# A conditioned two-block transformer layer stack: the first stage in the order of its data, and three weight pieces split a stage earlier

## The reference

```python
mod = silu(c) @ w_ada + b_ada            # 6 vectors of 1024, also for c_ctx
sh1, sc1, gt1, sh2, sc2, gt2 = split(mod, 6)
h  = rms_norm(x, g_norm1) * (1.0 + sc1) + sh1
hc = rms_norm(ctx, g_norm1) * (1.0 + csc1) + csh1
aq, ak, av, dq, dk, dv, dz, da, db, ga, gd = split_cols(h @ w_in)
...                                      # attention; gated delta rule, 12 steps, both directions
y_d = rms_norm(o_d, dn_norm_g) * silu(dz)
y = sigmoid(ga) * (y_a @ w_br_attn) + sigmoid(gd) * (y_d @ w_br_dn)
```

## Time and profile before

| | |
|---|---|
| runs shown | 2957.41, 2962.56, 5729.62 us; median 2962.56 |
| profiled execution | 2958.29 us, span 2956.3 |
| TensorE busy | 2718.9 us, 92% |
| VectorE, ScalarE busy | 49%, 30% |
| mean granted clock of TensorE | 0.96 of full |
| moved by DMA | 242.41 MB, mean 82 GB/s |

### The profile page before, as it was taken

The page is one execution under the profiler, slowest core; times in us unless marked ns, Lnnn a source line. Parts: engine busy times, 40 slices in busy tenths (PEclk is TensorE's granted clock), DMA queues, the critical chain, the costliest instruction groups (busy, mean ns, idle before and its releaser), DMA issues.

```text
span 2956.3 us, 48454 instructions
## 1 busy us (share of the span) xinstructions
PE 2718.9 (92%) x20908; PEld 2170.7 (73%) x20908; DVE 1444.9 (49%) x2474; ACT 892.1 (30%) x1516; POOL 87.2 (3%) x140
## 2 busy tenths in 40 slices
PE   3999988888889999998889899999999889899998
PEld 1767656667778778876767678888888666688876
DVE  2455556668853444434356653333334346544434
ACT  2434421110032333223335432222222335333322
POOL 0000011112200000000000000000000000000000
PEclk6999989999999999999899999999999899999999
DMA  6000356550023223222000212111210100222220
GB/s 250 30 29 29 130 186 230 206 189 3 3 87 121 86 86 110 90 86 82 29 29 29 86 37 78 58 57 58 80 63 29 39 29 29 114 89 111 86 86 29
DMA packets 17921, 242.41 MB, mean 82 GB/s; under 512 B 2016, under 2 KB 2176, under 8 KB 2864
## 3 DMA queue, kind: packets, MB, share of 16 engines
q1 hardware_dynamic: 16416, 231.94, 21.1%
q0 software_dynamic: 1296, 7.39, 0.6%
HBM read 237.23 MB, written 2.10 MB: 81 GB/s over the span
## 4 chain that ended last, share of the span: by engine, by line
PE 86%; DVE 8%; issue 2%; DMA 2%; ACT 2%; POOL 0%; DVEq 0%; ACTq 0%; SPq 0%; POOLq 0%
PE ps L333 57%; PE ps L1221 7%; PE ps L395 2%; PE ps L1778 2%; PE ps L1997 2%; PE ps L875 1%; PE ps L2025 1%; PE ps L2041 1%; PE ps L831 1%; DVE hh L486 1%; PE ps L2043 1%; PE ps L2042 1%; DMA cst<-in_consts 1%; PE ps L877 1%; PE ps L876 1%
## 5 line engine op out<-in xcount | busy, mean ns | idle before, releaser
L333 PE MATMUL ps<-hh,ws 128*128 128x512 f32 x3600 | 856.8, 397 | 39.1 <-DVE hh L486 27.0
L333 PEld LDWEIGHTS ps<-hh,ws 128*128 128x128 f32 x3600 | 679.8, 191 | 199.8 <-issue 46.9
L324 DVE TENSOR_TENSOR ws<-raw,ws 128x1024 fp32r<-128x1024 f32 x295 | 360.2, 1222 | 242.1 <-ACT ws L316 242.0
L316 ACT ACTIVATE ws<-raw 128x1024 fp32r<-128x1024 f32 x295 | 309.3, 1050 | 507.0 <-PE ps L333 433.2
L333 PE MATMUL ps<-g,ws 128*128 128x512 f32 x1536 | 364.5, 395 | 0.0
L333 PEld LDWEIGHTS ps<-g,ws 128*128 128x128 f32 x1536 | 286.1, 188 | 67.2
L1221 PEld LDWEIGHTS ps<-ar 64*64 64x64 f32 x6656 | 214.8, 141 | 52.5 <-issue 34.4
L1532 DVE SCALAR_TENSOR_TENSOR xT<-ps,mods,xT 128x512 f32<-128x512 f32 x120 | 90.1, 750 | 323.3 <-PE ps L333 323.3
L1221 PE MATMUL ps<-ar 64*64 64x64 f32 x6656 | 230.6, 226 | 18.0 <-issue 10.3
L333 PE MATMUL ps<-gg,ws 128*128 128x512 f32 x960 | 226.1, 395 | 0.0
L333 PEld LDWEIGHTS ps<-gg,ws 128*128 128x128 f32 x960 | 180.3, 188 | 43.7
(11 more groups left out here) (313 smaller groups left out, 2997.9 us busy)
## 6 DMA issues: line engine op xcount, KB each, us to landing
raw<-in_w_ada SPq DMA_DIRECT2D x36, 2048.0 KB, 8.6
raw<-in_w_m SPq DMA_DIRECT2D x32, 2048.0 KB, 7.8
raw<-in_w_mlp SPq DMA_DIRECT2D x16, 2048.0 KB, 7.7
raw<-in_w_in SPq DMA_DIRECT2D x8, 2048.0 KB, 7.8
raw<-in_w_mg SPq DMA_DIRECT2D x8, 1536.0 KB, 6.6
raw<-in_w_out SPq DMA_DIRECT2D x6, 2048.0 KB, 7.6
raw<-in_w SPq DMA_DIRECT2D x5, 2048.0 KB, 7.9
xT<-in_xT POOLq DMA_DIRECT2D x1, 2048.0 KB, 15.6
```

The source lines that it names most:

```text
L316: e.activation(w_of(n)[0], pieces[n][2], ACT.Copy).then_inc(*hi(n))
L324: e.tensor_tensor(l, pieces[n][2], h.bitcast(F32), ALU.subtract).then_inc(*lo(n))
L333: m = e.matmul(o, a, b, start=n == 0, stop=n == 3 * kt - 1)
```

## The change

It has two parts.

1. First stage. The identity gets a transfer of its own, second in POOL's queue; the transposes wait for that one. Each square of x and of the context goes to TensorE by itself: 8 + 8 products with ones take the place of 2 + 2 and of DVE's 12 additions, with four buffers in the place of two. x is squared on ACT, the context on DVE. The sums and squares stand between the modulation blocks. Piece 2 (`ab`) is split between the two norms instead of ahead of both.
2. Delta rule's end. ACT and DVE split the pieces `dz` 0 to 2 at the end of the delta stage; on DVE that is ahead of block 35's reduction.

```diff
-        come = {n: sig(f"in_{n}") for n in ("par1", "x", "cx", "cst", "par2", "cs1", "cst2", "cx2", "rope", "wpl",
+        come = {n: sig(f"in_{n}") for n in ("par1", "ident", "x", "cx", "cst", "par2", "cs1", "cst2", "cx2", "rope", "wpl",
...
             if i == 0:
-                e.wait_ge(*come["cst"]["in"])
+                e.wait_ge(*come["ident"]["in"])
...
         def pool_start(e):
             e.dma_start(par1[:, :], I["par1"]).then_inc(*come["par1"]("in", 16))
+            e.dma_start(C("ident"), I["consts"][:, 0:128]).then_inc(*come["ident"]("in", 16))
             e.dma_start(xT[:, :, :], I["xT"]).then_inc(*come["x"]("in", 16))
             e.memset(ones[:, :], 1.0).then_inc(*pool("ones"))
             e.memset(mi[:, 0:1], EPS).then_inc(*pool("eps"))
             e.memset(c32.rearrange("p k j -> p (k j)"), 0.0).then_inc(*pool(("c32", 0)))
             e.dma_start(cx, I["ctxT"]).then_inc(*come["cx"]("in", 16))
-            e.dma_start(cst[:, :], I["consts"]).then_inc(*come["cst"]("in", 16))
+            e.dma_start(cst[:, 128:CW], I["consts"][:, 128:CW]).then_inc(*come["cst"]("in", 16))
             e.dma_start(par2[:, :, :], I["par2"]).then_inc(*come["par2"]("in", 16))
             e.dma_start(cs1, I["rope1"]).then_inc(*come["cs1"]("in", 16))
 
+        first_squares = {"x1": (T, bufs_x), "c1": (TC, [ar[:, 9216 + i * 256:9472 + i * 256] for i in range(4)])}
+
+        def act_first_squares(e, ks):
+            for k in ks:
+                if k > 3:
+                    e.wait_ge(*acc["x1", "st", k - 4])
+                e.activation(bufs_x[k % 4], xT[:, k, :], ACT.Square).then_inc(*act(("x1", "sq", k)))
+
+        def dve_first_squares(e):
+            e.wait_ge(*come["cx"]["in"])
+            for k in range(KT):
+                if k > 3:
+                    e.wait_ge(*acc["c1", "st", k - 4])
+                e.tensor_tensor(first_squares["c1"][1][k % 4], cx[:, k, :], cx[:, k, :], ALU.mult).then_inc(
+                    *dve(("c1", "sq", k)))
+
+        def pe_first_sums(e, tag, sig_, ks):
+
+            n, bufs = first_squares[tag]
+            for k in ks:
+                if k == 0:
+                    for t in ps.take((tag, "st")):
+                        e.wait_ge(*t)
+                e.wait_ge(*sig_[tag, "sq", k])
+                e.matmul(ps[tag, "st"][:, 0:n], ones[:, :], bufs[k % 4], start=k == 0, stop=k == KT - 1).then_inc(
+                    *acc((tag, "st", k)))
+            acc.also((tag, "st"))
+
         def tensor_in(e):
-            for i in range(4):
-                pe_ada(e, i)
-                if i:
-                    pe_ada_t(e, i - 1)
+            pe_ada(e, 0)
+            pe_ada(e, 1)
+            pe_ada_t(e, 0)
+            e.wait_ge(*pool["ones"])
+            pe_first_sums(e, "x1", act, range(4))
+            pe_ada(e, 2)
+            pe_ada_t(e, 1)
+            pe_first_sums(e, "x1", act, range(4, 8))
+            pe_ada(e, 3)
+            pe_ada_t(e, 2)
+            pe_first_sums(e, "c1", dve, range(8))
             pe_ada_t(e, 3)
-            e.wait_ge(*pool["ones"])
-            pe_stat(e, "x1", T, rms_bufs(T))
-            pe_stat(e, "c1", TC, rms_bufs(TC))
+            e.wait_ge(*come["cst"]["in"])
 
         def scalar_in(e):
             table(e, SET_EXP_LN)
             act_c(e, 0)
-            for i in range(4):
-                act_ada(e, i)
+            act_ada(e, 0)
             e.wait_ge(*pool["eps"])
             e.wait_ge(*come["x"]["in"])
-            for k in range(KT):
-                act_square(e, "x1", k, xT[:, k, :], rms_bufs(T))
+            act_first_squares(e, range(4))
+            act_ada(e, 1)
+            act_first_squares(e, range(4, 8))
+            act_ada(e, 2)
             act_rms(e, "x1", T, rs[:, :])
-            e.wait_ge(*come["cx"]["in"])
-            for k in range(KT):
-                act_square(e, "c1", k, cx[:, k, :], rms_bufs(TC))
+            act_ada(e, 3)
             act_rms(e, "c1", TC, rsc)
-            split_hi(e, 2)
+            split_hi(e, 1)
             e.wait_ge(*dve["a1"])
             act_norm(e, "x1", sh1(0), hh, bufs_x)
+            split_hi(e, 2)
             act_norm(e, "c1", sh1(1), hc1, bufs_c)
 
         def vector_in(e):
             dve_c(e, 0)
-            for i in range(4):
+            dve_ada(e, 0)
+            dve_first_squares(e)
+            for i in range(1, 4):
                 dve_ada(e, i)
-            for tag, n in (("x1", T), ("c1", TC)):
-                for k in range(1, KT - 1):
-                    dve_square_sum(e, tag, k, rms_bufs(n))
             e.wait_ge(*dve["mod", 3])
             dve_gain(e, A1, mod, 1, 0, Q("gn1"))
             dve_gain(e, A1c, mod, 1, 1, Q("gn1"))
             dve.also("a1")
             e.wait_ge(*dve["a1"])
+            split_lo(e, 1)
+            dve_norm(e, "x1", xT, rs[:, :], gain1, sh1(0), hh, bufs_x)
             split_lo(e, 2)
-            dve_norm(e, "x1", xT, rs[:, :], gain1, sh1(0), hh, bufs_x)
+            e.wait_ge(*come["cst"]["in"])
             dve_norm(e, "c1", cx, rsc, gain1c, sh1(1), hc1, bufs_c)
 
 
@@ -1309,6 +1344,7 @@
                         dve_ada(e, a - 1)
                     if a == 11:
                         dve_c(e, 1)
+            split_lo(e, first["dz"] + 2)
             dve_ada(e, 35)
             e.wait_ge(*dve["mod", 11])
             dve_gain(e, A2, mod, 4, 0, Q("gn2"))
@@ -1394,6 +1430,7 @@
                     act_ada(e, a)
                     if a == 11:
                         act_c(e, 1)
+            split_hi(e, first["dz"] + 2)
 
         def gpsimd_delta(e):
             meet(e, pool, "tokens")
```

## The result

| | before | changed |
|---|---|---|
| median | 2962.52 us | 2937.07 us (2934.72 to 2941.89, 4 runs) |
| profiled execution | 2958.29, span 2956.3 | 2934.72, span 2932.9 |
| ratio | | 0.9922 [0.9902, 0.9942] |

The forecast was 2932 (2923 to 2948), from a gain of 28.1 us on the profiled execution of before. The profiled executions differ by 23.6 us, the medians by 25.4. One of the four executions of before took 5729.62 us; the ratio is that of the others. On other chips the kernel before had its median at 2958.94 and 2958.6; the changed kernel, once more, took 2936.85, ratio 0.9931 [0.9913, 0.9950].

The account below looks back on a forecast made before the run. TensorE, busy 92% of the span, was taken as the bound, its early and pre-merge waits set by a ScalarE/VectorE chain, constants and splits. 2958.3 - 22.3 - 5.8 = 2930.2, median 0 to 4 above: 2932 us, range 2923 to 2948.

Parts of the forecast that it names:

- Arrivals: First stage: x in by 19.0 us at the latest, up to 2.2 later behind the identity; block 3 at 33.1.
- TensorE's chain: First stage: transposes, sums and modulation blocks run from 22.8 us to the last context sum's end at 40.2.
- the one sum priced at the lower level: First x sums: one counted at TensorE's lower clock, 0.86 us extra, the clock rise being expected at 24 to 25.
- Rival B: First stage: clock stays low as short waits break up TensorE's work; total gain only 15 us, 2945; chance 0.13.
- rival E: First stage: FP32 sums cost far more than 0.86 to 1.72 us; at 4 us each 2970, slower; chance 0.03.
- Root, splits, norm: First stage after the last sum: norm of x at 44.6 instead of 67.4, gain 22.8, net 22.3 us.
- Delta rule's end: Merge start: earlier splits let TensorE begin at 815.2 instead of 820.95, gain 5.8 us; gap 10.2 to 4.4.
- The sum: Whole kernel: 2958.3 less 22.3 and 5.8 gives 2930.2 us; 2932 forecast as the median.
- What of it survives? ... I count no loss: After 70 us: each step waits for something that moves along, so the first stage's gain survives whole; loss none.
- Rival C: After the first stage: its gain is given back in a later wait, only the delta's end counts; 2954; chance 0.06.

Follow-up runs that it names:

- the padded kernels: Unused small products in TensorE's first-stage idle time: 208 instructions added to the changed kernel, 2925.69 us (0.9896); 48 added to the kernel before, 2971.91 us (1.0044).

## Why the prediction was right

- **Arrivals.** x took 16.8 us from its issue at 2.46, so it came at 19.3, 0.3 later than my latest. Before it had come at 17.5 (1.93 and 15.6), so the identity's transfer ahead of it cost 1.7 us, where the estimate in the prediction was up to 2.2; the identity itself took 7.5 us to land. Block 3 came at 33.6 against 33.1, for which TensorE waited 0.17. Nothing moved on that.
- **TensorE's chain.** Computed 23.9, 28.2, 30.8, 34.2, 36.8, 40.2 for the starts of the five pieces behind the first transposes and the end of the last; measured 24.0, 27.5, 29.9, 33.65, 36.0, 39.6. The 0.5 to 0.9 too much is the one sum priced at the lower level: the clock rose at about 24, ahead of the sums. Rival B didn't come, and rival E's price is excluded by the sums issued twice.
- **Root, splits, norm.** Computed 4.4 us from the last sum to the norm, measured 4.3 (39.6 to 43.9). The third split was computed at 0.5 us on the path and cost 0.3 (23.4 gained ahead of it, 23.1 behind). Net 23.1 against 22.3.
- **Delta rule's end.** Idle time 4.4 computed, 4.29 measured; gain 5.9 against 5.8. It ended at VectorE's gain, as said. The closeness is in part luck, as two misses cancel: the three lower halves took 4.01 in the place of 3.50, and block 35's reduction, addition and gain 0.45 in the place of 0.8. The clock fell all the same, and rose within 806; no gain from it, as taken.
- **The sum.** 28.1 computed, 23.6 measured in the profiles, 25.4 in the first medians and 22 in the next. The mechanism of both parts was right. The step that failed is "What of it survives? ... I count no loss". Rival C was there, with 0.06, and with the reason that no wait after 70 is fixed in time. That reason holds for waits on data. It misses what depends on the number of instructions: 49 more of them move every block end to other work. This term was 0 in my sum and is about 4 us in stalls and, with the clock, 8 in the profiled pair; the padded kernels put it at 11 to 13 in the medians. With the block ends held in place, the change is worth more than I said: 2958.94 to 2925.69, 33 us. This last figure flatters it a little: the padded kernel's stage took 416.5 us against 420.4 before, of which 2.5 are fewer waits for VectorE.
- **Range.** It held, as the pieces were exact and the loss was smaller than what rival B had left room for; that was luck, not insight into the loss.

## What to carry to other kernels

Give each consumer of an early load its own transfer, in the order of use, and put sums where an idle engine can do them as data arrive; then count that engine's chain piece by piece, which here came within 1 us over 20. Where TensorE has many short instructions and large transfers run beside them, compare two versions with their instruction counts brought to the same place in a block of 256, or a real gain of a few microseconds is hidden by a chance one. Look at every idle time put down to "issue": divide its instruction's number by 256, and look whether a packet of the instruction queue lands just ahead of its end.

## What was not expected of the hardware

- In the delta stage TensorE stood still 0.2 to 3.2 us at some of the places 256 instructions apart (remainder 192 to 196), nearly always behind large weight loads: 11.6 us in all before, 15.5 in the changed kernel, 2.7 with small loads. It went on 1.20 to 1.61 us after a packet of 16384 bytes of instructions had landed, in 115 of 118 cases.
- 208 useless instructions made the changed kernel 11 us faster; 48 made the kernel before 13 us slower.
- Such a stall can cost twice: after the one at 509.65 the clock was at 0.50. The time at the lower level in the delta stage was 47.7 to 78.5 us over 14 traces, and 51.2 and 60.8 in two of one kernel.
